# Four small products of pooled sums, from whole fp32 to three products of high and low parts

## The reference, cut to what matters

```
for g, w in enumerate((2, 4, 8, 16)):
    win_sum = c[:, 1:] - jnp.take(c, lo, axis=1)
    outs.append(win_sum / count[None, :, None] - pg[:, :, g])
d = jnp.stack(outs, axis=2).astype(p.dtype)
y = jnp.einsum('btgc,gcd->btgd', d, w_pool).reshape(B, T, POOL_WIDTH)
return y * pool_scale
```

## Time and profile before

| | us |
|---|---|
| median of 3 runs | 2756.87 |
| lowest, highest | 2756.3, 2759.5 |
| the profiled execution | 2758.08 |
| its span (first to last instruction) | 2756.3 |
| TensorE busy in it | 2735.3 |
| VectorE busy | 1820.9 |
| ScalarE busy | 1338.3 |
| GpSimd busy | 76.0 |

### The profile page before, as it was taken

One profiled execution on the slowest core, in us unless ns is written; L12 is line 12 of the kernel. 1 busy time (PEld: TensorE's weight loads), 2 busy tenths in 40 slices (PEclk: granted clock), 3 DMA queues, 4 the chain that ended last, 5 costly groups with the idle time before them and its releaser, 6 DMA issues.

```text
span 2756.3 us, 35298 instructions
## 1 busy us (share of the span) xinstructions
PE 2735.3 (99%) x14290; PEld 2272.5 (82%) x14290; DVE 1820.9 (66%) x2304; ACT 1338.3 (49%) x1606; POOL 76.0 (3%) x61
## 2 busy tenths in 40 slices
PE   9999999999999999999999999999999999999998
PEld 7888887888888888887888888888888888888887
DVE  6778855575556655766679754868667546656575
ACT  6566554664444434445545545544454444444443
POOL 0000000100000000000002000000010000000000
PEclk9999999999999999999999999999999999999999
DMA  8545455556555556554655556665655555565554
GB/s 326 206 161 169 153 192 175 175 188 203 195 190 190 200 194 192 194 187 161 224 177 178 182 180 209 191 213 176 207 196 191 195 195 194 183 204 190 195 190 160
DMA packets 145395, 529.21 MB, mean 192 GB/s; under 512 B 16288, under 2 KB 16720, under 8 KB 144592
## 3 DMA queue, kind: packets, MB, share of 16 engines
q1 hardware_dynamic: 142240, 514.45, 56.4%
q0 software_dynamic: 2560, 12.07, 1.2%
q10 hardware_dynamic: 432, 0.43, 0.1%
HBM read 524.78 MB, written 2.11 MB: 191 GB/s over the span
## 4 chain that ended last, share of the span: by engine, by line
PE 95%; DVE 2%; ACT 1%; issue 1%; DMA 0%; POOL 0%; DVEq 0%; SPq 0%; POOLq 0%; ACTq 0%
PE PS L579 95%; PE PS L582 1%; DVE RL L1684 1%; ACT RH L1172 1%; ACT A_HL L1172 1%; DVE AR L1684 0%; ACT SP L1172 0%; DVE AR L2157 0%; DMA RAW<-in_stream 0%; DVE X L1690 0%; ACT B_HL L1172 0%; DVE AR L1907 0%; DVE A_HL L1690 0%; POOL ST L2438 0%; DVE AR L1687 0%
## 5 line engine op out<-in xcount | busy, mean ns | idle before, releaser
L1684 DVE TENSOR_TENSOR RL<-RAW,RH 128x1024 fp32r<-128x1024 f32 x954 | 1159.2, 1224 | 828.8 <-ACT RH L1172 826.4
L1172 ACT ACTIVATE RH<-RAW 128x1024 fp32r<-128x1024 f32 (+1 forms) x962 | 1013.4, 1057 | 1128.4 <-PE PS L579 1096.2
L579 PE MATMUL PS<-RH,A_HL 128*128 128x512 f32 x4096 | 1270.9, 391 | 5.9 <-ACT RH L1172 2.2
L579 PEld LDWEIGHTS PS<-RH,A_HL 128*128 128x128 f32 x4096 | 767.8, 188 | 170.8 <-issue 6.2
L579 PE MATMUL PS<-RH,B_HL 128*128 128x512 f32 x2624 | 810.2, 390 | 0.4 <-DVE RL L1684 0.3
L579 PE MATMUL PS<-RL,A_HL 128*128 128x512 f32 x2048 | 792.1, 390 | 0.0
L579 PEld LDWEIGHTS PS<-RH,B_HL 128*128 128x128 f32 x2624 | 492.3, 188 | 104.1 <-DVE RL L1684 1.3
L579 PE MATMUL PS<-RL,B_HL 128*128 128x512 f32 x1312 | 508.7, 389 | 0.0
L579 PEld LDWEIGHTS PS<-RL,A_HL 128*128 128x128 f32 x2048 | 384.7, 188 | 78.6
L579 PEld LDWEIGHTS PS<-RL,B_HL 128*128 128x128 f32 x1312 | 246.1, 188 | 50.6
L579 PE MATMUL PS<-A_HL,RH 128*128 128x512 f32 (+1 forms) x912 | 219.6, 393 | 0.0
(11 more groups left out here) (122 smaller groups left out, 847.3 us busy)
## 6 DMA issues: line engine op xcount, KB each, us to landing
RAW<-in_stream SPq DMA_DIRECT2D x960, 512.0 KB, 4.2
X<-in_x SPq DMA_DIRECT2D x4, 512.0 KB, 7.7
AR<-in_mem SPq DMA_DIRECT2D x4, 512.0 KB, 6.9
AR<-in_mem_turned SPq DMA_DIRECT2D x4, 512.0 KB, 4.8
AR<-in_b_branch_gates POOLq DMA_DIRECT2D x4, 512.0 KB, 5.7
AR<-in_b_branch_gates POOLq DMA_DIRECT2D x2, 1024.0 KB, 9.0
out_x<-X SPq DMA_DIRECT2D x8, 256.0 KB, 2.7
AR<-in_x_turned SPq DMA_DIRECT2D x3, 512.0 KB, 8.9
```

The costliest lines, as they stand in the source:

```text
L579: return g.matmul(o, l, r, start=start, stop=stop, skip_group_check=True)
L1172: return g.activation(o, i, f, bias=bias, scale=scale, accum_out=accum)
L1684: return g.tensor_tensor(o, a, b, f)
```

## The change

WINDOW + n in the diff is slot n of this text. Both operands of the four products are now split into a high and a low part first. Four pieces of 512 columns of B_HL (`pooled(w, 0)` to `pooled(w, 3)`: map high, map low, sums high, sums low; chunks 8 to 15, two sets in turn) take them. ScalarE makes the two high parts of a group, VectorE the two low parts, TensorE does three fp32r matmuls in place of each float32 one. The groups follow each other at a distance of 1.5 slots instead of 1, and TensorE takes them at slots 13, 14.5, 16 and 17.5 instead of 16 to 19. The evictions of group w - 1 are put into the same generators as the parts of group w.

```diff
+        s_wph, s_wpl = sem("window_high_made"), sem("window_low_made")
...
+        pooled = lambda w, k: BV[:, 4096 + 2048 * (w % 2) + 512 * k:4608 + 2048 * (w % 2) + 512 * k].rearrange("p (k n) -> p k n", k=2)
...
             def pool_task():
                 for w in range(4):
-                    yield WINDOW + 16 + w
-                    g.wait_ge(s_wp, 16)
-                    g.wait_ge(s_pw, 3 * w + 3)
+                    yield WINDOW + 13 + 1.5 * w
+                    g.wait_ge(s_wpl, 2 * w + 2)
                     if w > 1:
                         g.wait_ge(s_plo, w - 1)
                     b = 4 + w % 2
                     for c in range(2):
                         for kc in range(2):
-                            t = mm(PS[:, b, c * T:c * T + T], WP[:, w, kc, c * P:c * P + P], windows[w][:, 2 * w + kc, :],
-                                   c == 0 and kc == 0, kc == 1)
+                            cs, o = slice(c * P, c * P + P), PS[:, b, c * T:c * T + T]
+                            w_high, w_low, s_high, s_low = [pooled(w, k)[:, kc, :] for k in range(4)]
+                            mm(o, w_low[:, cs], s_high, c == 0 and kc == 0, False)
+                            mm(o, w_high[:, cs], s_low, False, False)
+                            t = mm(o, w_high[:, cs], s_high, False, kc == 1)
                     t.then_inc(s_pmm, 1)
...
             def pool_task():
-                for w in range(4):
-                    yield WINDOW + 17 + w
+
+                def evict(w):
                     g.wait_ge(s_pmm, w + 1)
                     for c in range(2):
                         t = act(BH[:, 2 * w + c, :], PS[:, 4 + w % 2, c * T:c * T + T], scale=gcol("pool_scale_2", 2 * w + c))
                     t.then_inc(s_phi, 1)
+
+                for w in range(4):
+                    yield WINDOW + 11 + 1.5 * w
+                    g.wait_ge(s_wp, 16)
+                    if w > 1:
+                        g.wait_ge(s_pmm, w - 1)
+                    act(pooled(w, 0), WP[:, w, :, :]).then_inc(s_wph, 1)
+                    g.wait_ge(s_pw, 3 * w + 3)
+                    act(pooled(w, 2), windows[w][:, 2 * w:2 * w + 2, :]).then_inc(s_wph, 1)
+                    if w:
+                        yield WINDOW + 11.5 + 1.5 * w
+                        evict(w - 1)
+                yield WINDOW + 18.5
+                evict(3)
...
+                def low(w):
+                    g.wait_ge(s_phi, w + 1)
...
+                    t.then_inc(s_plo, 1)
+
                 for w in range(4):
-                    yield WINDOW + 10 + w
+                    yield WINDOW + 10 + 1.5 * w
...
-                for w in range(4):
-                    yield WINDOW + 17 + w
-                    g.wait_ge(s_phi, w + 1)
...
-                    t.then_inc(s_plo, 1)
+                    yield WINDOW + 11.5 + 1.5 * w
+                    g.wait_ge(s_wph, 2 * w + 1)
+                    tt(pooled(w, 1), WP[:, w, :, :], pooled(w, 0).bitcast(F32), ALU.subtract).then_inc(s_wpl, 1)
+                    g.wait_ge(s_wph, 2 * w + 2)
+                    tt(pooled(w, 3), s[:, cs, :], pooled(w, 2).bitcast(F32), ALU.subtract).then_inc(s_wpl, 1)
+                    if w:
+                        yield WINDOW + 12 + 1.5 * w
+                        low(w - 1)
+                yield WINDOW + 19
+                low(3)
...
                 yield WINDOW + 20.5
-                g.wait_ge(s_pmm, 4)
+                g.wait_ge(s_wpl, 8)
                 rows(U(7), 1024, 2, s_brow[1])
```

More of the change, by code:

```diff
@@ L2054, in pool_task @@
                 pv = by_head(PP)
+                def low(w):
+                    g.wait_ge(s_phi, w + 1)
+                    for c in range(2):
+                        t = stt(BL[:, 2 * w + c, :], PS[:, 4 + w % 2, c * T:c * T + T], gcol("pool_scale_2", 2 * w + c),
+                                BH[:, 2 * w + c, :].bitcast(F32), ALU.mult, ALU.subtract)
+                    t.then_inc(s_plo, 1)
                 for w in range(4):
-                    yield WINDOW + 10 + w
+                    yield WINDOW + 10 + 1.5 * w
                     s, cs = windows[w], slice(2 * w, 2 * w + 2)
@@ L2067, in pool_task @@
                     tt(s[:, cs, 0:16], tmp, pv[:, cs, 0:16], ALU.subtract).then_inc(s_pw, 1)
-                for w in range(4):
-                    yield WINDOW + 17 + w
-                    g.wait_ge(s_phi, w + 1)
-                    for c in range(2):
-                        t = stt(BL[:, 2 * w + c, :], PS[:, 4 + w % 2, c * T:c * T + T], gcol("pool_scale_2", 2 * w + c),
-                                BH[:, 2 * w + c, :].bitcast(F32), ALU.mult, ALU.subtract)
-                    t.then_inc(s_plo, 1)
+                    yield WINDOW + 11.5 + 1.5 * w
[8 more added lines that the diff above has]
+                low(3)
             def scores_task():
```

## The result

| | before | changed |
|---|---|---|
| median of 22 runs, us | 2758.16 | 2761.82 |
| lowest, highest | 2756.3, 2759.5 | 2759.69, 2765.0 |
| span of the profiled execution | 2756.3 | 2760.0 |

The ratio is 1.0015, 95% interval 1.0009 to 1.0021: 3.7 us slower, where +3.3 was forecast. The time lies in the stated range and inside the 0.2% (5.5 us), on the slow side, though the upper end of the interval touches it. Of the 1.6 us between the 2760.2 of the forecast and the 2761.82 measured, 1.3 come from the starting value: 22 runs of the kernel before have their median at 2758.16, where the first three had 2756.87.

What follows compares the result with a forecast made beforehand. TensorE was taken as the bound, busy in 99% of the span. Products -1.2 us, waits +2.1 and +2.4, made +3.3 us: 2760.2 us beside 2756.87, range 2755 to 2764.5.

Steps and rivals of the forecast that it cites:

- The products, -1.2 us: On TensorE, twelve fp32r matmuls at 0.119 us cost 1.43 us a group instead of 1.74, saving 1.2 us in all.
- Rival (c): On TensorE, weight loads don't overlap matmuls, so a group costs some 2.5 us; 2761.2 us in all, chance 0.03.
- The price of a split: Each 128 x 512 high split on ScalarE and low subtraction on VectorE was taken to cost 0.62 us.
- Rival (b): Half-size splits cost what whole ones do, 1.2 us on VectorE and 1.06 on ScalarE; 2764.8 us, chance 0.14.
- The walk: New order followed: TensorE doesn't wait before groups 0 and 1, waits 2.1 us before group 2, 2.4 before 3.
- The split of the loss: TensorE's waiting for parts was forecast as 2.1 us before group 2 and 2.4 us before group 3.
- Nothing behind slot 20: TensorE would begin slot 20 near 1523 with 3.4 us to spare; the earlier bias transfer would cost nothing.
- Rival (a), the cover holds: TensorE never waits for the parts: 2755.7 us, or 2757.9 with one wait left; chance 0.25 for both.

Runs made afterwards that it cites:

- the run with one filler: Changed kernel plus 14 more fp32r matmuls by 256 columns where TensorE waits for the parts of group 2; 55.47 us from slot 9 to 24, ratio 1.0017.

## Why the prediction was right

- *The products, -1.2 us.* Right: 12 matmuls stood from 1494.52 to the next one at 1495.96, 0.12 apart, and the products alone gave -1.18. The weight loads do overlap the matmuls here: one load and one matmul take 0.475 us together by the medians of their records (shortest, median and longest in ns below), four times the distance.

```profile
L581 PEld LDWEIGHTS PS<-B_HL x48: 186/192/335, 1494.3 to 1516.7; 128*128 128x128 f32 x48
L581 PE MATMUL PS<-B_HL x48: 277/283/419, 1494.5 to 1516.9; 128*128 128x256 f32 x48
```

  The trace thus disagrees with the rule of the Trainium skill ("TensorE: Matmul & The Clock Gate", section "Part 3: Packing small matmuls — row/col tiling") that I set aside in the prediction; by it, as an estimate, the same run would have been 3.3 us longer. Rival (c) is out. Its 2.5 us a group were called a price in rows, but no row shows them.
- *The price of a split.* 0.62 us was taken for both engines. A pair of VectorE's takes 1.21 to the start of what follows (1506.19 to 1507.40), 0.60 each; ScalarE's take 0.63. Rival (b) is out. Its own terms (2.3, 0.9 and 1.2) add up to 4.4, where the prediction has 4.6.
- *The walk.* Group 0 and 1: no wait, seen. Slot 17 on ScalarE at 1500.3 (1500.6 in the walk, which started 0.15 us later), lows of group 2 at 1507.5 (1507.8), of group 3 at 1515.4 (1515.9). The waits stand before groups 2 and 3 and nowhere else.
- *The split of the loss.* Here a step was off in form. I had 2.1 and 2.4 us of waiting, 4.5 in all. It is 1.9, then 1.7 of half clock, then 0.7 start to start, 4.3 in all. I had not asked what a wait does to the clock. The sum is nearly the same because the last of the three ends when the parts of group 3 come. That the half clock fell where a wait followed was luck: in the run with one filler it fell one wait later and cost 1.5.
- *Nothing behind slot 20.* Right: the changed kernel's TensorE has no wait from the product of group 3 to slot 24, and slots 24 to 32 took 23.17 us in both. The bias transfer cost nothing visible.
- *Rival (a), the cover holds,* did not happen in the changed kernel, but it was possible and only a matter of order: the runs with the sums early are it.

## What to carry to other kernels

A third of an engine's time left free (VectorE's here, by the page) doesn't tell whether new work fits; its place in the order does. Where two engines hand pieces to each other in program order, walk the order by hand with measured durations, and look for a piece that stands behind something that the other engine has to wait for: moving 2 us of VectorE's work (the sums of two groups) to an earlier place gave back 3.8 of the 4.4 us that adding 10 us of work had cost, and half a slot for one product the rest. And where single executions differ by more than the change, compare a fixed stretch between two marks of the trace: it repeated to 0.02 us where the totals spread by 3 to 5.

## What the runs showed of the hardware

- After a TensorE wait of 1.77 us the granted clock was 0.50 for 3.4 us in both profiles of the changed kernel, from 1 us behind the wait. In the one-filler run it came 1 us behind a wait of 2.10. But waits of 1.21 and 1.80 us (all but the products) and of 1.05 and 2.10 us (evictions later) were followed by none before slot 24. In the kernel before, the wait of 2.2 us that ends near 1287 was followed by it at once in one execution and not in the other. So a wait of some 2 us can be followed by it and need not, with the same program; what decides was not tried.
- One execution of the kernel with the evictions later took 7112.91 us, its other nine 2760.58 to 2762.81. In its trace TensorE is busy in 100 of 100 us, and a matmul by 512 columns takes 829 ns instead of 391 by its record. They start some 0.6 us apart, where the changed kernel has 0.23, and 0.43 in its stretch at half clock. VectorE's split of a slot takes 1.225 us there and 1.224 in the changed kernel. The granted clock reads 1.00, but it does so even in the last 11 us, where TensorE is busy for only 2.7 and the other traces show it lower; so this 1.00 may mean no more than that no change of the clock was recorded. The cause is open.
